# A two-layer encoder trunk: VectorE's first residual add moved ahead of the last operands, and the third up unit computed by token halves

## The reference, cut to what matters

```
def squared_relu_mlp(h, w_up, w_down):          # w_up (1024, 4096), w_down (4096, 1024)
    return jnp.square(jax.nn.relu(h @ w_up)) @ w_down

for layer in range(2):
    h = rms_norm(x, norm_mix[layer])
    y = conv_rwkv_mixer(h, ...) if layer % 2 == 0 else swa_sink_mixer(h, ...)
    x = x + y
    x = x + squared_relu_mlp(rms_norm(x, norm_mlp[layer]), mlp_up[layer], mlp_down[layer])
```

## Time and profile before

| | |
|---|---|
| Median of 3 runs | 2557.21 us (2549.19 to 2566.81) |
| Profiled execution, its own time | 2564.11 us |
| Its span, first to last instruction | 2562.3 us |
| PE busy, share of the span | 2389.2 us, 93% |
| DVE / ACT / POOL busy | 1406.4 / 783.3 / 408.0 us |
| Mean granted TensorE clock | 0.957 |

### The profile page before, as it was taken

How to read it: one execution, slowest core, us unless ns; L and a number is a source line. 1 busy time by engine, 2 the same in 40 slices (tenths; PEclk the granted TensorE clock), 3 DMA queues, 4 the chain that set the end, 5 groups by cost and what they waited for, 6 DMA issues and landing times.

```text
span 2562.3 us, 41341 instructions
## 1 busy us (share of the span) xinstructions
PE 2389.2 (93%) x16338; PEld 1941.9 (76%) x16338; DVE 1406.4 (55%) x1958; ACT 783.3 (31%) x1226; POOL 408.0 (16%) x405
## 2 busy tenths in 40 slices
PE   6999979998999999999999799788999999999998
PEld 5888867877777787778778688445778777877787
DVE  3344467676336546655655532674265665566555
ACT  5011035344123322332233122463142233223323
POOL 0000021111231010101110600232411111111110
PEclk8999979899999999999999899899999999999999
DMA  3221100001111111111111111000111111111112
GB/s 110 66 87 48 42 2 4 3 3 44 34 41 49 42 57 49 41 49 57 44 46 49 36 50 41 1 1 25 41 42 58 49 41 49 57 49 41 49 49 82
DMA packets 166156, 110.85 MB, mean 43 GB/s; under 512 B 3598, under 2 KB 163684, under 8 KB 166052
## 3 DMA queue, kind: packets, MB, share of 16 engines
q1 hardware_dynamic: 163756, 100.39, 13.1%
q0 software_dynamic: 2240, 8.91, 1.1%
q10 hardware_dynamic: 56, 0.01, 0.0%
HBM read 102.49 MB, written 6.29 MB: 42 GB/s over the span
## 4 chain that ended last, share of the span: by engine, by line
PE 79%; DVE 10%; issue 5%; ACT 2%; POOL 1%; DMA 0%; DVEq 0%; SPq 0%; POOLq 0%; ACTq 0%
PE ps L278 42%; PE ps L383 22%; PE ps L952 2%; DVE t_lo L668 1%; PE ps L974 1%; PE ps L1660 1%; DVE probs L1688 1%; PE ps L333 1%; DVE softmax_stats L1693 1%; DVE stage L664 1%; DVE b_raw L661 1%; PE ps L1003 1%; DVE w_sums_lo L672 1%; ACT b_raw L575 1%; PE ps L1474 1%
## 5 line engine op out<-in xcount | busy, mean ns | idle before, releaser
L278 PE MATMUL ps<-h_hi,w_hi 128*128 128x512 f32 x1568 | 490.1, 394 | 31.4 <-DVE h_lo L521 17.7
L278 PE MATMUL ps<-h_lo,w_hi 128*128 128x512 f32 x1568 | 486.5, 392 | 0.0
L278 PE MATMUL ps<-h_hi,w_lo 128*128 128x512 f32 x1568 | 485.3, 391 | 0.0
L233 ACT CAST w_hi<-w_raw 128x1024 fp32r<-128x1024 f32 x180 | 189.3, 1052 | 946.9 <-PE ps L278 720.1
L679 DVE TENSOR_TENSOR residual<-residual,ps 128x512 f32<-128x512 f32 x448 | 300.2, 686 | 200.0 <-PE ps L383 199.8
L278 PEld LDWEIGHTS ps<-h_hi,w_hi 128*128 128x128 f32 x1568 | 294.0, 189 | 94.7 <-issue 13.3
L278 PEld LDWEIGHTS ps<-h_lo,w_hi 128*128 128x128 f32 x1568 | 296.5, 189 | 62.7
L278 PEld LDWEIGHTS ps<-h_hi,w_lo 128*128 128x128 f32 x1568 | 296.2, 189 | 62.4
L237 DVE TENSOR_TENSOR w_lo<-w_raw,w_hi 128x1024 fp32r<-128x1024 f32 x180 | 222.1, 1234 | 29.5 <-ACT w_hi L233 29.4
L647 POOL TENSOR_TENSOR w_sums_raw<-w_raw 128x256 f32<-128x256 f32 x64 | 47.3, 740 | 1172.3 <-DMA w_raw<-in_mlp_down 656.2
L383 PE MATMUL ps<-t_hi,w_sums_hi 128*128 128x512 f32 x384 | 157.3, 410 | 46.3 <-DVE residual L679 46.3
(11 more groups left out here) (295 smaller groups left out, 3775.4 us busy)
## 6 DMA issues: line engine op xcount, KB each, us to landing
w_raw<-in_mlp_up SPq DMA_DIRECT2D x64, 512.0 KB, 4.0
w_raw<-in_mlp_down SPq DMA_DIRECT2D x64, 512.0 KB, 3.4
w_raw<-in_w_in_ab SPq DMA_DIRECT2D x26, 512.0 KB, 3.8
w_raw<-in_w_qkv SPq DMA_DIRECT2D x10, 512.0 KB, 3.9
x_in_tile<-in_x POOLq DMA_DIRECT2D x8, 512.0 KB, 4.2
w_raw<-in_w_out_ab SPq DMA_DIRECT2D x8, 512.0 KB, 3.6
w_raw<-in_w_o SPq DMA_DIRECT2D x8, 512.0 KB, 3.7
out<-out_chunk SPq DMA_DIRECT2D x8, 512.0 KB, 3.2
```

What stands on the lines that cost most here:

```text
L233: nc.scalar.copy(WH[:, slot], WR[:, slot]).then_inc(w_hi, 1)
L278: m = nc.tensor.matmul(acc(a_slot, half), ww, xx[:, k, half * HALF:(half + 1) * HALF], start=first, stop=last)
```

## The change

Unit 2 is now computed by token halves as unit 3 was, and its operands are made in two parts by the same loop: half 1 gives b22_0, t2_0, t3_0, then half 0 gives b21_0 and t4_0. The relu, the square and the two splits of unit 2 that each covered 1024 elements become two instructions of 512 each. `split_hi` and `split_lo` of the first down unit (u + 4) stand behind unit 2's last operand instead of ahead of its first; `sums_hi(1)` follows there on ACT, and `sums_lo(0)` comes before unit 2's relu on DVE. At the end of unit 3, DVE's add of p1_0 stands directly behind the last relu, ahead of `t4_1`; the add of p5_0 stands ahead of `lo` of b21_1; the add of p6_0 ahead of `lo` of t4_1. PE's order of units and products is unchanged apart from the order of matmuls within unit 2.

```diff
-        squares = Track("relu_squared", ["r0", "r1", "r2", "r3b", "r3a"])
+        squares = Track("relu_squared", ["r0", "r1", "r2b", "r2a", "r3b", "r3a"])
...
-            def up_by_halves(g):
-                t.wait_ge(w_lo, u0 + 8 * g + 3 + 3)
-                t.wait_ge(acc_free[1], a0_ // 2 + 2 * g + 1 + 1)
+            def up_by_halves(g, j):
+                slot = j - 2
+                t.wait_ge(w_lo, u0 + 8 * g + j + 3)
+                t.wait_ge(acc_free[slot], a0_ // 2 + 2 * g + 1 + 1)
...
-                for j in range(3):
+                for j in range(2):
                     up(g, j, between if j == 0 else None)
-                up_by_halves(g)
+                up_by_halves(g, 2)
+                up_by_halves(g, 3)
...
             sums_hi(0)                                   # mlp_act
+            for c in range(2):
+                act.wait_ge(half_staged, 2 * G + (c + 1))
+                square(B2R[:, 1, c], f"r{2 + c}b")
+                sums_dve.wait(act, G, f"t2_{c}")
+                hi(M2H[:, c], R[c][:, T1H], f"t2_{c}")
+                hi(B2H[:, 1, c], B2R[:, 1, c], f"b22_{c}")
+                sums_dve.wait(act, G, f"t3_{c}")
+                hi(M3H[:, c], M3R[:, c], f"t3_{c}")
+                act.wait_ge(acc_free[c], a0_ // 2 + 2 * g + 3)
+                square(B2R[:, 0, c], f"r{2 + c}a")
+                squares.wait(act, G, f"r{2 + c}a")
+                hi(B2H[:, 0, c], B2R[:, 0, c], f"b21_{c}")
+                sums_dve.wait(act, G, f"t4_{c}")
+                hi(M4H[:, c], M4R[:, c], f"t4_{c}")
+                if c == 0:
+                    split_hi(act, 0, n + 2, ag + 5)
+                    sums_hi(1)
...
             sums_lo(0)                                   # mlp_dve
+            for c in range(2):
+                dve.wait_ge(half_done, 2 * G + (c + 1))
+                relu(b22[c], acc(c, 1), RI[:, T1H]).then_inc(half_staged, 1)
+                squares.wait(dve, G, f"r{2 + c}b")
+                combine(R[c][:, T1H], b22[c], R[c][:, T1H], f"t2_{c}")
+                sums_dve.wait(dve, G, f"t2_{c}")
+                combine(m3[c], R[c][:, T1H], R[c][:, T0H], f"t3_{c}")
+                lo(M2L[:, c], R[c][:, T1H], M2H[:, c], f"t2_{c}")
+                lo(B2L[:, 1, c], b22[c], B2H[:, 1, c], f"b22_{c}")
+                lo(M3L[:, c], m3[c], M3H[:, c], f"t3_{c}")
+                dve.wait_ge(acc_done, ag + 2 + c + 3)
+                relu(b21[c], acc(c, 0), RI[:, T0H]).then_inc(acc_free[c], 1)
+                if c:
+                    add("p1_0", 0, 0, 4)
+                squares.wait(dve, G, f"r{2 + c}a")
+                combine(m4[c], b21[c], R[c][:, T1H], f"t4_{c}")
+                if c:
+                    add("p5_0", 1, 1, 7)
+                sums_dve.wait(dve, G, f"t4_{c}")
+                lo(B2L[:, 0, c], b21[c], B2H[:, 0, c], f"b21_{c}")
+                if c:
+                    product_6(0)
+                lo(M4L[:, c], m4[c], M4H[:, c], f"t4_{c}")
+                if c == 0:
+                    split_lo(dve, 0, u + 4)
             sums_lo(1)
             split_lo(dve, 1, u + 5)
```

More of the change, by code:

```diff
@@ L310, in hybrid_trunk @@
         dn_dve = Track("down_added", DOWN)
-        squares = Track("relu_squared", ["r0", "r1", "r2", "r3b", "r3a"])
+        squares = Track("relu_squared", ["r0", "r1", "r2b", "r2a", "r3b", "r3a"])
         sums_dve = Track("operand_sums", ["t1_0", "t1_1", "t2_0", "t3_0", "t4_0", "t2_1", "t3_1", "t4_1"])
-        OPERANDS = ["t1_0", "b11_0", "t1_1", "b11_1", "b2_0", "t2_0", "t3_0", "t4_0", "t2_1", "b22_1", "t3_1", "b21_1",
-                    "t4_1"]
+        OPERANDS = ["t1_0", "b11_0", "t1_1", "b11_1", "t2_0", "b22_0", "t3_0", "b21_0", "t4_0",
+                    "t2_1", "b22_1", "t3_1", "b21_1", "t4_1"]
         op_hi = Track("operands_hi", OPERANDS)
-        op_lo = Track("operands_lo", ["t1_0", "b11_0", "t1_1", "b11_1", "t2_0", "b2_0", "t3_0", "t4_0", "t2_1", "b22_1", "t3_1",
-                                      "b21_1", "t4_1"])
+        op_lo = Track("operands_lo", OPERANDS)
         half_done, half_staged = sem("last_up_half_done"), sem("last_up_half_staged")
@@ L366, in up @@
                         ready=(h_lo, 8 * H_FILL[f"mlp{l}"]) if j == 0 else None, between=between)
-            def up_by_halves(g):
-                t.wait_ge(w_lo, u0 + 8 * g + 3 + 3)
-                t.wait_ge(acc_free[1], a0_ // 2 + 2 * g + 1 + 1)
+            def up_by_halves(g, j):
+                slot = j - 2
+                t.wait_ge(w_lo, u0 + 8 * g + j + 3)
+                t.wait_ge(acc_free[slot], a0_ // 2 + 2 * g + 1 + 1)
                 for half in (1, 0):
                     for k in range(8):
-                        w_h, w_l = WH[:, 1, k * P:k * P + P], WL[:, 1, k * P:k * P + P]
+                        w_h, w_l = WH[:, slot, k * P:k * P + P], WL[:, slot, k * P:k * P + P]
                         for ww, xx in ((w_h, Hh), (w_h, Hl), (w_l, Hh)):
                             first, last = k == 0 and ww is w_h and xx is Hh, k == 7 and ww is w_l
-                            m = nc.tensor.matmul(acc(1, half), ww, xx[:, k, half * HALF:(half + 1) * HALF],
+                            m = nc.tensor.matmul(acc(slot, half), ww, xx[:, k, half * HALF:(half + 1) * HALF],
                                                  start=first, stop=last)
@@ L711, in mlp_dve @@
             m3, m4 = ([m[:, c] for c in range(2)] for m in (M3R, M4R))
-            dve.wait_ge(acc_done, ag + 2 + 3)
-            relu(B2R[:, :, 0], acc(0), RI[:, :].rearrange("p (h n) -> p h n", h=2)).then_inc(acc_free[0], 1)
             sums_lo(0)
[L715 to L744, removed]
+            for c in range(2):
[23 more added lines that the diff above has]
+                    split_lo(dve, 0, u + 4)
```

## The result

The changed kernel takes 2475.98 us (median of 4 runs, 2465.81 to 2487.63) against 2562.01 us for the kernel before (4 runs, 2549.19 to 2571.63: the three behind the 2557.21 us of the table above, and one of 2571.63): ratio 0.967, 95% interval 0.960 to 0.973. That is 86 us less by the medians; the two profiled executions differ by 2564.11 - 2479.71 = 84.4 us.

What follows compares the result with a forecast made beforehand. PE was taken to bound the kernel, standing still at p6_0 for a queued DVE add. Removing 78.3 us over 16 groups gave 2485.8 (profiled) or 2478.9 (median), middle 2482; 8-in-10 range 2466 to 2510.

Steps and rivals of the forecast that it cites:

- What bounds: PE, busy 93% of the span; p6_0 starts 3.08 us late, waiting for p1_0's add queued behind three DVE instructions.
- The sum: Loss in the MLP groups: 68.5 us in 14, 4.9 us each (3.08 stall, 1.8 clock); 78.3 us for all 16.
- The forecast of 2482: Whole kernel's time with the 78.3 us loss removed; the forecast had chance 0.74 and spanned 2466 to 2500.
- two estimates: Whole kernel's time less 78.3 us: 2485.8 from the profiled execution, 2478.9 from the median.
- The clock: TensorE drops to 1.2 GHz after PE's stall at p6_0, losing 1.8 us a group; the change removes this.
- rival 2: At p6_0 only the standing still goes, the clock falls for another reason: 49 us won, 2512 us; chance 0.03.
- What is late next: After p6_0's stall goes, no new PE stall; split_lo(1, u + 5) before p1_1 tightest, at most 2 us in all.
- POOL: POOL's sums beside DVE's unit 2 subtracts: three subtracts each wait up to 0.74 us, 1.7 us in all, covered.
- cover: Delay DVE's chain from unit 2 to p1_0's add can take before that add is late: about 2.1 us.
- Rival 1: Part of the stall stays, at p6_0 through POOL or at p1_1: 2496 us, 2510 with half the clock's loss; chance 0.16.
- Rival 4: Slower: p1_1 waits for split_lo(1, u + 5); 4 us a group gives 2572, longer clock fall 2590; chance 0.03.
- break-even: A stall of 3.1 us at p1_1 with the same fall of the clock would cancel the gain.

Runs made afterwards that it cites:

- e1: The kernel before with only DVE's adds moved forward, unit 2 left whole: 2498.95 us, ratio 0.975 to before.
- e2: The changed kernel with the adds back in their old places, unit 2 still by halves: 2495.53 us, ratio 0.974 to before.
- e3: The changed kernel with the add of p1_0 one instruction later, behind t4_1: 2478.7 us, ratio 0.967 to before.
- e4: The changed kernel with the first three adds behind sums_lo(1): 2534.0 us, ratio 0.990 to before.
- e7: The changed kernel with the first three adds behind the operands' low parts, ahead of sums_lo(1): 2510.8 us, ratio 0.979 to before.
- e8: The changed kernel with the first three adds behind sums_lo(1) and split_lo(1, u + 5): 2576.9 us, ratio 1.005 to before.
- e5: The changed kernel with POOL making four more sums of the second down unit ahead of the real four: 2481.61 us in one run.
- e6: The changed kernel with POOL making eight more sums of the second down unit ahead of the real four: 2518.55 us in one run.

## Why the prediction was right

- *What bounds.* PE's stall at p6_0, held by the place of one add in DVE's queue. Shown: the changed kernel and six others with the add at another place or time (e1, e2, e3, e4, e7, e8) have the stall that the queue gives, to 0.05 us.
- *The sum.* 68.5 us for fourteen groups, measured 68.7. For the two last groups 9.8 us were taken, as if they lost the mean of 4.9 us. They lost 14.22 - 8.16 = 6.1 and 14.11 - 8.16 = 5.9 us, as the groups at clock 0.96 do, and 11.8 us show in the two stretches. So the change is worth some 80.5 us; the profiles differ by 84.4 because of 3.9 us of chance ahead of the MLPs.
- *The forecast of 2482, measured 2476.* That it came so near is in part luck. It lies between two estimates, for the reason that part of the spread of the runs was the clock's fall, which the change removes. The runs don't bear that out: they spread over 22.4 us before and 21.8 us after. The start of the first MLP alone varies by 21 us between the profiles, and a fall of the clock costs only 1.6 to 2.8 us.
- *The clock.* Right for this kernel: 1.00 in all groups, so rival 2 is out. I hadn't weighed that half of the change would be enough for it; e1 and e2 show that.
- *What is late next.* Nothing, as counted. The add at 1.56 us behind p1_0, split_lo 0.32 us ahead of p1_1 (0.32 counted).
- *POOL.* DVE's delay was 0.96 us and not 1.7: two subtracts met a sum and not three, and lost 0.42 and 0.54 us, less than the 0.74 of a sum. The cover is 2.2 us, as e5 shows. Rival 1 would need much more of POOL's work than there is: four more sums leave no stall (e5), eight more bring one (e6). The Trainium skill's rule (SBUF — State Buffer, "Who interferes with whom"), that a two-input DVE instruction and a reading GpSimd instruction exclude each other for the whole instruction, agrees in its kind: both sides get longer only where they meet, from 0.69 to 1.23 us and from 0.74 to 1.09 us. But a subtract and a sum together take 1109.30 - 1108.15 = 1.15 us in e5, and not 0.60 + 0.74 = 1.34, so durations as the profile counts them overlap in part.
- *Rival 4.* The break-even was put at a stall of 3.1 us, and one of 4 us at 2572 to 2590. e8, with 3.98 us at p6_0 and not at p1_1, is at 2577, slower by 0.5%. So the price of such a stall was right; one at p1_1 was not made.

## What to carry to other kernels

When the tensor engine waits for a short instruction on another engine, look at what is queued ahead of it there: moving that one instruction forward costs nothing where the ones that it passes have time to spare, and the sizes of the rows already told the new start to within 0.1 us here. Two edits that shorten the same stall don't add: value the second by what the first leaves, and count the clock's loss as a step that goes away with the long stall. To see effects of a few us in a kernel whose runs spread by 20, compare the period of the repeated stage in the profiles, not the medians.

## What was not expected of the hardware

The loss beside the stall isn't proportional to the stall: 0.1 to 0.2 us a group behind 0.29 to 1.71 us of standing still, at clock 1.00 throughout, then 0.90 behind 2.84, 1.83 behind 3.07, 2.26 behind 3.98. Between 2.84 and 3.07 us this mean doubles, because the clock fell in 12 of the 14 groups and not in 7, and in 4 of them the costlier way (clock 0.96). The stall was the same to 0.1 us in all whole groups of a kernel; what decides which of them falls, and how, wasn't tried. Where DVE and POOL shared time in the MLPs, a subtract of 512 elements took up to 1.23 us, its own 0.69 and most of one sum, and none in the rows read was held for two.
